# Two-block transformer on one core: the second w_out unit split during the forget-gate attention, the third unit's load issued before the recurrence

## The chip, the cores and the metric

One NeuronCore of one Trainium2 chip. The metric is the device time of one execution in microseconds (us); lower is better. The kernel before: 2402.63 us, median of three runs (2399.54, 2402.63, 2403.07).

## What is computed

Two blocks in sequence over 512 tokens of width 1024, in float32. The part that the change touches is the mixer of the first block:

```python
proj = hn @ w_in[l]
...
fox_out = fox_attention(to_heads(fq), to_heads(fk), to_heads(fv), log_f)   # 8 heads of 64, causal, forget gates
rec = hgrn2_chunkwise(gq, gf, gi, lbs[l])                                  # 4 heads of 128, gated recurrence
rec = rmsnorm(rec, hgrn_norm_g[l]) * silu(gg)
h = h + concatenate([fox_out, rec], axis=-1) @ w_out[l]                    # "out": 4 units of 256 columns
mem_n = rmsnorm(mem, norm_mem_g[l])                                        # 256 memory rows
h = h + memory_cross_attention(rmsnorm(h, norm_x_g[l]), mem_n, w_xq[l], w_xkv[l], w_xo[l])
```

After that come a squared-ReLU MLP, and the second block: pooling with grid attention, an mLSTM, and two gated MLPs.

## The kernel before, in words

Every large product runs on TensorE in three passes. A weight w is split into wH, its rounded copy, and wL = w - wH; the activation likewise (hnH and hnL, or uH and uL). `parts` (L1680) issues wH·xH, wH·xL and wL·xH. The weights are cut by `plan()` (L46) into 161 **units**, most of 1024 x 256. Units 0 to 14 are w_in (stage "in"), units 15 to 18 are w_out (stage "out"), and unit 19 is the first of w_xkv. Unit n uses buffers number n % 2 of `raw`, `wH` and `wL`, and goes through four steps on four engines:

- `load(n)`, SP (L405): a DMA of 1 MB into `raw`, once `low(n - 2)` is done, since that was the last reader of the buffer.
- `high(n)`, ACT (L610): waits for the load and for TensorE to have finished unit n - 2 (`blk_done`); copies `raw` into `wH`.
- `low(n)`, POOL (L507): waits for `high(n)`; wL = raw - wH.
- TensorE (L1691): `unit_ready` (L1687) waits for `high(n)` and `low(n)`, then come 48 matmuls of 128x512 in two blocks. DVE takes each block from PSUM.

Each engine runs its own instruction stream in order. The order in which a stream places `high`, `low` and `load` among its other work is written by hand. Around the change the order is this:

- TensorE: units 0 to 14, `attention("fox")` (L1769), the recurrence (L1886 on), unit 15, unit 16, four transposes of the normalized memory rows, unit 17, four transposes, unit 18, and then w_xkv.
- `attention("fox")` is a software pipeline of steps s = 0 to 31 (head s // 4, query block s % 4 of 128 rows), plus a drain. In step s, TensorE computes the scores of s (L1787, L1789), transposes the probabilities of s - 3 (L1836), and after each fourth step multiplies a head's probabilities with its values (L1814, eight matmuls, "values of head h"). DVE takes the row maximum of s (L1094, L1098), then scales the probabilities of s - 1 (L1103, L1104). ACT does the exponential of s (L683), and copies the transposed probabilities of s - 3 (L702) and the gates (L672). Between these, DVE prepares the recurrence through `gate_steps` (L1174): among this are four cumulative sums (L1187, TENSOR_TENSOR_SCAN), one per step from step 21 on.
- The recurrence uses PE, DVE, ACT and POOL (L527 to L536). It ends with the DVE operation that makes the last `uL` (L1029); this is counted in `op_lo`.
- SP: loads 0 to 15, then a wait for `op_lo` at the end of the attention, the table `lvl` (L441), a wait for `op_lo` at the end of the recurrence, the memory rows `mtok` (L445), and then loads 16 on (L446).
- POOL: `low(0)` to `low(15)` (L519), the recurrence, `low(16)` on (L537).
- ACT: `high(0)` to `high(15)`, the attention, the recurrence, `high(16)` (L765), the memory statistics (L766 to L769), `high(17)` (L770), `high(18)` with the memory chunks.

So unit 15 is ready long before it is used, and unit 16 is loaded and split while TensorE works on unit 15.

Of the kernel before, what the change touches and what calls it, by code (L numbers as in the profile page):

```python
# [109 lines left out]
UNITS, AT = plan()  # L110
# [58 lines left out]
def add(i, count):  # L169

    return count if i is None else i + count


def outputs(kind, t):

    h = t // TB
    if t % TB != TB - 1 or not 0 <= h < ATT[kind]["heads"]:
        return []
    return [2 * h, 2 * h + 1] if kind == "cross" else [h // 2] if h % 2 else []


def bass_block_pair(nc, a, out):
# [155 lines left out]
    with ExitStack() as ctx:  # L338
# [65 lines left out]
        def _(sp):  # L404
            def load(n, value=None, src=None):  # L405


                w, k0, kc, c0, c, _ = UNITS[n]
                if n >= 2:
                    sp.wait_ge(w_lo, (n if value is None else value) - 1)  # L410
                if src is None:
                    src = weight_view(w)[:, k0:k0 + kc, c0:c0 + c]
                sp.dma_start(raw[n % 2][:, 0:kc, 0:c], src).then_inc(raw_in[n % 2], 16)

            def loads(first, last):
                for n in range(first, last):
                    load(n)
# [19 lines left out]
            sp.dma_start(gbias[96:128, :], a["od_gate_b_2"].rearrange("a b -> b a")).then_inc(vec_in, 16)  # L437
            loads(0, AT["out"][0] + 1)

            sp.wait_ge(op_lo, Q0["mix"] + 4)  # L440
            sp.dma_start(lvl[:], a["levels"].rearrange("l s t -> s l t")).then_inc(lvl_in, 16)  # L441

            sp.wait_ge(op_lo, Q0["mix"] + 8)
            for mb in range(2):
                sp.dma_start(mtok[:, mb, :], a["mem"][0, mb * P:(mb + 1) * P, :]).then_inc(mem_in, 16)  # L445
            loads(AT["out"][0] + 1, AT["ff1"][0])  # L446

            def load_ada(layer, i, m):

# [56 lines left out]
        def _(pool):  # L506
            def low(n, value=None):  # L507

                _, _, kc, _, c, _ = UNITS[n]
                pool.wait_ge(w_hi, (n if value is None else value) + 1)  # L510
                nc.gpsimd.tensor_tensor(wL[n % 2][:, 0:kc, 0:c], raw[n % 2][:, 0:kc, 0:c],  # L511
                                        wH[n % 2][:, 0:kc, 0:c].bitcast(F32), ALU.subtract).then_inc(w_lo, 1)

            def lows(first, last):
                for n in range(first, last):
                    low(n)


            lows(0, AT["out"][0] + 1)  # L519

            v = 0
            for h in range(HG_H):
                for l in range(len(HG_LEVELS)):
# [8 lines left out]
                    if l == 3:  # L532
# [1 line left out]
                        if h:  # L534
                            pool.wait_ge(h_kt, h)
                        nc.gpsimd.tensor_tensor(kd[:], gk[:, h, :], ed[:], ALU.mult).then_inc(h_kd, 1)  # L536
            lows(AT["out"][0] + 1, AT["ff1"][0])  # L537
            n0 = AT["ff1"][0]
            with pool.Fori(0, 4) as i:
                for u in range(8):  # L540
# [60 lines left out]
        def _(act):  # L601
# [8 lines left out]
            def high(n, i=None, du=0, db=0):  # L610


                if n >= N_UNITS:
                    return
                _, _, kc, _, c, _ = UNITS[n]
                act.wait_ge(raw_in[n % 2], add(None if i is None else i * (8 * du), 16 * (n // 2 + 1)))
                if n >= 2:
                    act.wait_ge(blk_done, add(None if i is None else i * db, BLOCK0[n - 1]))
                nc.scalar.activation(wH[n % 2][:, 0:kc, 0:c], raw[n % 2][:, 0:kc, 0:c], ACT.Copy).then_inc(w_hi, 1)  # L619
# [39 lines left out]
            def attention(kind):  # L659
                c = ATT[kind]  # L660
                ns = c["heads"] * TB
                width = {"fox": None, "cross": M_MEM, "grid": S}[kind]
                for s in range(ns + 7):
                    g = c["step0"] + s
                    if kind == "fox":

                        h = 0 if s == 0 else (s + 2) // 4 if s % 4 == 2 else FOX_H
                        if h < FOX_H:
                            act.wait_ge(f_bc, h + 1)
                            if h >= 2:  # L670
                                act.wait_ge(mx_done, 4 * (h - 1))
                            nc.scalar.activation(fbc[h % 2][:], ps[2 + h % 2][:], ACT.Copy).then_inc(f_bcs, 1)  # L672
                    if s < ns:
                        i = s % TB
                        w = (i + 1) * P if kind == "fox" else width
                        act.wait_ge(mx_done, g + 1)
                        if kind == "fox":
                            src = pr[g % PR_RING][:, 0:w]
                        else:
                            src = ps[4 + g % 2][:, 0:w]  # L680
                            act.wait_ge(tp_done, g - PR_RING + 1)
                        m = g % PR_RING
                        nc.scalar.activation(pr[m][:, 0:w], src, ACT.Exp, bias=nmax[:, m:m + 1],  # L683
                                             accum_out=rsum[:, m:m + 1]).then_inc(ex_done, 1)
                    if kind == "fox" and s == 8:

                        act.wait_ge(blk_taken, TAKEN[BLOCK0[AT["out"][0]]])
                        nc.scalar.activation(gq[:], gq[:], ACT.Silu).then_inc(h_act, 1)
                        nc.scalar.activation(gg[:], gg[:], ACT.Silu).then_inc(h_act, 1)
                        nc.scalar.activation(gk[:], gk[:], ACT.Sigmoid).then_inc(h_act, 1)  # L690
                    if kind == "fox" and s == 16:
                        for hh in range(HG_H):
                            act.wait_ge(h_fk, hh + 1)
                            nc.scalar.activation(lnf[:, hh, :], lnf[:, hh, :], ACT.Ln).then_inc(h_ln, 1)
                    t = s - 3
                    if 0 <= t < ns:
                        h, i = t // TB, t % TB
                        nj = (i + 1) if kind == "fox" else width // P
                        act.wait_ge(tp_done, c["step0"] + t + 1)
                        if i == 0 and h >= 2:  # L700
                            act.wait_ge(pv_done, c["pv0"] + c["pvh"] * (h - 1))
                        nc.scalar.activation(pT[h % 2][:, 0:nj, i * P:(i + 1) * P],  # L702
                                             ps[6 + (c["step0"] + t) % 2][:, 0:nj * P].rearrange("p (j t) -> p j t", j=nj),
                                             ACT.Copy).then_inc(pt_done, 1)

                    for o in outputs(kind, s - 5):
                        act.wait_ge(pv_done, c["pv0"] + (o + 1 if kind == "cross" else 2 * o + 2))
                        nc.scalar.activation(uH[:, c["col0"] + o, :], ps[o % 2][:], ACT.Copy).then_inc(op_hi, 1)
# [14 lines left out]
            for u, n in enumerate(range(*ranges("in"))):  # L723
                high(n + 1)
                if u == 8:
# [4 lines left out]
                    nc.scalar.activation(frow[1][:], frow[1][:], ACT.Ln, bias=ones[0:FOX_H, 0:1]).then_inc(f_l, 1)  # L730

            attention("fox")

            v = 0
# [27 lines left out]
                high_op(Q0["mix"] + 4 + h, uH[:, 4 + h, :], T[h % 2][:], (op_t, tq[0]))  # L762

            n = AT["out"][0]
            high(n + 1)  # L765
            act.wait_ge(mem_in, 32)  # L766
            for mb in range(2):
                chain(nc.scalar.activation(mdump[:], mtok[:, mb, :], ACT.Square, accum_out=mstat[:, mb:mb + 1]))
            nc.scalar.activation(mstat[:, 4:6], mstat[:, 0:2], ACT.Sqrt, bias=eps, scale=1.0 / D).then_inc(m_root, 1)  # L769
            high(n + 2)  # L770
            for half in range(2):
                high(n + 3 + half)
                for j in range(4 * half, 4 * half + 4):
# [4 lines left out]
            n = AT["xkv"][0]  # L778
# [8 lines left out]
            for n in range(*ranges("xq")):  # L787
                high(n + 1)
            attention("cross")
            for n in range(*ranges("xo")):  # L790
                high(n + 1)
# [34 lines left out]
            n = AT["ev_in"][0]  # L826
# [22 lines left out]
            for j in range(2):  # L849
                act.wait_ge(g_dup, j + 1)  # L850
                nc.scalar.activation(kdup[:, j, :], ps[(7, 4)[j]][:], ACT.Copy).then_inc(g_kd, 1)
            attention("grid")
            for j in range(4):
                tq[0] += 1
# [46 lines left out]
            n = AT["od_in"][0]  # L901
# [1315 lines left out]
```

## Time and profile before

| what | us |
|---|---|
| median of three runs | 2402.63 |
| lowest and highest run | 2399.54, 2403.07 |
| profiled execution, first to last instruction (its span) | 2398.8 |
| PE busy | 2172.8 |
| DVE, POOL, ACT busy | 1170.9, 845.5, 707.7 |

Each run gives one number for the whole execution. The profiled execution has its span of 2398.8 us; no separate device time is listed for it. The median of the runs is 3.8 us above the span. Times in the rows below are from the start of the span. PE is TensorE, and its granted clock is shown as a share of 2.4 GHz: 1.00 is the upper level of 2.4 GHz, 0.50 the lower of 1.2 GHz.

### The profile page before, as it was taken

Reading aid. Unit: us, or ns where it says so; the run is one execution under the profiler, and the core shown is the slowest. Engines: PE = TensorE matmul, PEld = TensorE weight load, DVE = VectorE, ACT = ScalarE, POOL = GpSimd, SP = SyncE. Lnnn points to the kernel's source line nnn. Section 1 sums busy time; section 2 is a strip of 40 time slices with the busy share of each in tenths; the row PEclk is TensorE's granted clock in tenths of the full one; section 3 lists DMA queues with packets and bytes.
Section 4 is the critical chain, followed back from the end, with each engine's and each line's share of the span. In section 5 each row is a group of like instructions: output and inputs, shape, how many; then the busy total and the mean of one; then the engine's idle time right before and its main releaser. Section 6 shows DMA issues by size and latency. Waiting matters only on the chain.

```text
span 2398.8 us, 26469 instructions
## 1 busy us (share of the span) xinstructions
PE 2172.8 (91%) x10170; PEld 1732.0 (72%) x10170; DVE 1170.9 (49%) x1876; ACT 707.7 (30%) x938; POOL 845.5 (35%) x303
## 2 busy tenths in 40 slices
PE   6998857899889999979987999999799878999998
PEld 5884356786668788867346888888698556888887
DVE  4113695553288887463535676632456654111112
ACT  3124522333332221333433212222233332313221
POOL 2441062451324443323212443344233323344442
PEclk8997878899989999989898999999899988999999
DMA  4320001241345553312004555522232002233322
GB/s 133 97 88 0 9 1 53 89 140 53 123 136 180 175 175 125 103 53 101 0 18 140 176 176 178 189 88 88 80 96 71 1 1 88 88 97 97 98 90 75
DMA packets 220414, 226.12 MB, mean 94 GB/s; under 512 B 3787, under 2 KB 218524, under 8 KB 220188
## 3 DMA queue, kind: packets, MB, share of 16 engines
q1 hardware_dynamic: 220316, 224.78, 28.8%
q8 instruction: 65, 1.06, 0.2%
q14 instruction: 33, 0.27, 0.0%
HBM read 222.67 MB, written 2.10 MB: 94 GB/s over the span
## 4 chain that ended last, share of the span: by engine, by line
PE 76%; DVE 11%; issue 7%; ACT 4%; POOL 1%; DMA 1%; DVEq 0%; SPq 0%; ACTq 0%; POOLq 0%
PE ps L1683 22%; PE ps L1685 21%; PE ps L1684 21%; PE ps L1814 2%; PE ps L1794 1%; DVE ssum L995 1%; ACT wH L619 1%; DVE adacc L1361 1%; DVE ssum L992 1%; PE ps L1836 1%; PE ps L1898 1%; PE ps L1787 1%; PE ps L1750 1%; DVE small L1009 1%; PE ps L1805 1%
## 5 line engine op out<-in xcount | busy, mean ns | idle before, releaser
L511 POOL TENSOR_TENSOR wL<-raw,wH 128x2048 fp32r<-128x2048 f32 (+2 forms) x161 | 729.6, 4533 | 1308.1 <-ACT wH L619 1308.1
L1683 PE MATMUL ps<-hnH,wH 128*128 128x512 f32 x1336 | 530.5, 397 | 20.2 <-DVE hnL L1031 9.9
L1684 PE MATMUL ps<-hnL,wH 128*128 128x512 f32 x1336 | 525.2, 393 | 0.0
L1685 PE MATMUL ps<-hnH,wL 128*128 128x512 f32 x1336 | 525.0, 393 | 0.0
L619 ACT ACTIVATE wH<-raw 128x2048 fp32r<-128x2048 f32 (+2 forms) x161 | 302.4, 1879 | 673.7 <-PE ps L1685 653.6
L1683 PE MATMUL ps<-uH,wH 128*128 128x512 f32 x864 | 342.2, 396 | 13.7 <-DVE uL L1029 9.8
L1684 PE MATMUL ps<-uL,wH 128*128 128x512 f32 x864 | 338.9, 392 | 0.0
L1685 PE MATMUL ps<-uH,wL 128*128 128x512 f32 x864 | 338.9, 392 | 0.0
L1683 PEld LDWEIGHTS ps<-hnH,wH 128*128 128x128 f32 x1336 | 254.2, 190 | 75.1 <-issue 23.3
L1685 PEld LDWEIGHTS ps<-hnH,wL 128*128 128x128 f32 x1336 | 254.1, 190 | 54.3
L1684 PEld LDWEIGHTS ps<-hnL,wH 128*128 128x128 f32 x1336 | 254.4, 190 | 52.6 <-issue 0.5
L1361 DVE SCALAR_TENSOR_TENSOR adacc<-adaw,small,adacc 128x256 f32<-128x256 f32 x336 | 278.8, 830 | 12.0
L1683 PEld LDWEIGHTS ps<-uH,wH 128*128 128x128 f32 x864 | 163.8, 190 | 49.5 <-issue 13.6
L1487 DVE TENSOR_TENSOR T<-ps,R 128x512 f32<-128x512 f32 x44 | 30.4, 692 | 325.0 <-PE ps L1685 325.0
L1685 PEld LDWEIGHTS ps<-uH,wL 128*128 128x128 f32 x864 | 163.8, 190 | 34.8
L1684 PEld LDWEIGHTS ps<-uL,wH 128*128 128x128 f32 x864 | 163.9, 190 | 33.4
L1076 DVE SCALAR_TENSOR_TENSOR xT<-ps,mod,xT 128x512 f32<-128x512 f32 x64 | 47.4, 750 | 183.8 <-PE ps L1685 183.8
L1683 PE MATMUL ps<-wH,hnH 128*128 128x256 f32 (+1 forms) x416 | 117.7, 283 | 2.9 <-issue 2.9
L1684 PE MATMUL ps<-wL,hnH 128*128 128x256 f32 (+1 forms) x416 | 117.5, 282 | 0.0
L1685 PE MATMUL ps<-wH,hnL 128*128 128x256 f32 (+1 forms) x416 | 117.4, 282 | 0.0
L1390 DVE TENSOR_TENSOR uL<-T,uH 128x512 fp32r<-128x512 f32 x32 | 84.6, 2681 | 21.6 <-ACT uH L812 21.6
L879 ACT ACTIVATE uH<-T 128x512 fp32r<-128x512 f32 x44 | 27.8, 633 | 190.2 <-DVE T L1487 190.2
(330 smaller groups left out, 2524.5 us busy)
## 6 DMA issues: line engine op xcount, KB each, us to landing
raw<-in_ffn_w_dram SPq DMA_DIRECT2D x60, 1024.0 KB, 5.3
adaw<-in_ada_w_dram SPq DMA_DIRECT2D x48, 1024.0 KB, 7.3
raw<-in_w_dram SPq DMA_DIRECT2D x32, 1024.0 KB, 5.2
raw<-in_w_in_dram SPq DMA_DIRECT2D x14, 1024.0 KB, 5.4
raw<-in_od_w_in_dram SPq DMA_DIRECT2D x12, 1024.0 KB, 5.3
raw<-in_w_xkv_dram SPq DMA_DIRECT2D x8, 1024.0 KB, 5.2
raw<-in_ffn_w_dram SPq DMA_DIRECT2D x8, 768.0 KB, 4.2
raw<-in_ev_w_in_dram SPq DMA_DIRECT2D x5, 1024.0 KB, 5.3
```

The costliest lines, as they stand in the source:

```text
L511: nc.gpsimd.tensor_tensor(wL[n % 2][:, 0:kc, 0:c], raw[n % 2][:, 0:kc, 0:c], wH[n % 2][:, 0:kc, 0:c].bitcast(F32), ALU.subtract).then_inc( ...
L619: nc.scalar.activation(wH[n % 2][:, 0:kc, 0:c], raw[n % 2][:, 0:kc, 0:c], ACT.Copy).then_inc(w_hi, 1)
L879: nc.scalar.activation(uH[:, 2 * p + c, :], T[(q0 + c) % 2][:], ACT.Copy).then_inc(op_hi, 1)
L992: nc.vector.tensor_copy(acc[:], sq[q % 2][:]).then_inc(sq_added, 1)
L1076: nc.vector.scalar_tensor_tensor(out=xT[:, j, :], in0=ps[b % 4][:], scalar=gate(j), in1=xT[:, j, :], op0=ALU.mult, op1=ALU.add).then_inc(b ...
L1361: ins = nc.vector.scalar_tensor_tensor(out=acc, in0=adaw[m % ADA_RING][:, k, :], scalar=condc[:, k:k + 1], in1=acc, op0=ALU.mult, op1=ALU.add)
L1390: nc.vector.tensor_tensor(uL[:, 2 * u + c, :], T[q % 2][:], uH[:, 2 * u + c, :].bitcast(F32), ALU.subtract).then_inc(op_lo, 1)
L1487: nc.vector.tensor_tensor(T[(q0 + c) % 2][:], ps[b % 4][:], R[c][:], ALU.mult).then_inc(blk_taken, 1)
L1683: nc.tensor.matmul(out_ap, wh, xh, start=first, stop=False)
L1684: nc.tensor.matmul(out_ap, wh, xl, start=False, stop=False)
L1685: return nc.tensor.matmul(out_ap, wl, xh, start=False, stop=last)
L1814: ins = nc.tensor.matmul(ps[h // 2 % 2][hp:hp + 64, t0:S], v, pT[h % 2][:, j, t0:S], start=(j == 0), stop=(j == TB - 1))
```

## The change

SP issues loads 16 and 17 right behind load 15, ahead of its two waits for the attention and for the recurrence. ACT does `high(16)` in the attention, at step 20, behind the exponential of that step; behind the recurrence it does `high(17)` at once, ahead of the memory statistics instead of behind them. POOL does `low(16)` behind `low(15)`, ahead of the recurrence's operations.

```diff
@@ SP
             loads(0, AT["out"][0] + 1)
 
+            load(AT["out"][0] + 1)
+            load(AT["out"][0] + 2)
             sp.wait_ge(op_lo, Q0["mix"] + 4)
...
-            loads(AT["out"][0] + 1, AT["ff1"][0])
+            loads(AT["out"][0] + 3, AT["ff1"][0])
@@ POOL
-            lows(0, AT["out"][0] + 1)
+            lows(0, AT["out"][0] + 2)
...
-            lows(AT["out"][0] + 1, AT["ff1"][0])
+            lows(AT["out"][0] + 2, AT["ff1"][0])
@@ ACT, in attention()
+                    if kind == "fox" and s == 20:
+                        high(AT["out"][0] + 1)
                     if kind == "fox" and s == 16:
@@ ACT, behind the recurrence
             n = AT["out"][0]
-            high(n + 1)
+            high(n + 2)
             act.wait_ge(mem_in, 32)
...
-            high(n + 2)
             for half in range(2):
                 high(n + 3 + half)
```

Two lines are added above ACT's and POOL's code, so line numbers of the changed kernel are 2 to 4 higher there.

ACT in the attention, from the exponential of step 20 (`pr_86`) to that of step 21 (`pr_87`). Before:

```order
L683 ACTIVATE pr_86,small<-pr_86,small 128x128
L702 ACTIVATE pT_90<-ps 128x2x128
L708 ACTIVATE uH<-ps 128x512
L683 ACTIVATE pr_87,small<-pr_87,small 128x256
L702 ACTIVATE pT_90<-ps 128x3x128
```

With the change:

```order
L685 ACTIVATE pr_86,small<-pr_86,small 128x128
L621 ACTIVATE wH_51<-raw_49 128x2048
L706 ACTIVATE pT_90<-ps 128x2x128
L712 ACTIVATE uH<-ps 128x512
L685 ACTIVATE pr_87,small<-pr_87,small 128x256
L706 ACTIVATE pT_90<-ps 128x3x128
```

The copy of unit 16 stands between the two exponentials, ahead of a copy of transposed probabilities and of one `uH`.

ACT behind the recurrence, from its last `uH`. Before:

```order
L645 ACTIVATE uH<-T_69 128x512
L619 ACTIVATE wH_51<-raw_49 128x2048
L768 ACTIVATE mdump,small<-mtok 128x1024 x2
L769 ACTIVATE small<-small 128x2
L619 ACTIVATE wH_52<-raw_50 128x2048
L619 ACTIVATE wH_51<-raw_49 128x2048
```

With the change:

```order
L647 ACTIVATE uH<-T_69 128x512
L621 ACTIVATE wH_52<-raw_50 128x2048
L772 ACTIVATE mdump,small<-mtok 128x1024 x2
L773 ACTIVATE small<-small 128x2
L621 ACTIVATE wH_51<-raw_49 128x2048
```

`high(16)` (`wH_51`) is gone from here, and `high(17)` (`wH_52`) stands ahead of the memory statistics.

POOL, from `low(14)` to the first operations of the recurrence. Before:

```order
L511 TENSOR_TENSOR wL_53<-raw_49,wH_51 128x2048
L511 TENSOR_TENSOR wL_54<-raw_50,wH_52 128x2048
L527 TENSOR_TENSOR kt_106<-gk,R_70 128x512
L527 TENSOR_TENSOR kt_107<-gk,R_71 128x512
```

With the change:

```order
L513 TENSOR_TENSOR wL_53<-raw_49,wH_51 128x2048
L513 TENSOR_TENSOR wL_54<-raw_50,wH_52 128x2048
L513 TENSOR_TENSOR wL_53<-raw_49,wH_51 128x2048
L529 TENSOR_TENSOR kt_106<-gk,R_70 128x512
L529 TENSOR_TENSOR kt_107<-gk,R_71 128x512
```

`low(16)` is the third row: it now stands ahead of the recurrence.

## Rows read from the trace of the kernel before

**Rows 1.** The page: the span, and the chain that ended last, by engine

```profile
span 2398.8 us, 26469 instructions
...
PE 76%; DVE 11%; issue 7%; ACT 4%; POOL 1%; DMA 1%; DVEq 0%; SPq 0%; ACTq 0%; POOLq 0%
```

**Rows 2.** PE timeline, unit 15 to unit 16 (start, us, operation, [idle before <- releaser])

```profile
419.10 0.39 PE L1683 MATMUL ps<-uH,wH 128*128 128x512 f32 x1
...
421.60 0.39 PE L1685 MATMUL ps<-uH,wL 128*128 128x512 f32 x1
424.21 0.61 PE L1683 MATMUL ps<-uH,wH 128*128 128x512 f32 x1 [2.22 <-ACT wH L619]
424.62 0.63 PE L1684 MATMUL ps<-uL,wH 128*128 128x512 f32 x1
...
436.80 1.04 PE L1943 MATMUL ps<-cst,mtok 128*128 128x128 f32 x8
```

**Rows 3.** SP timeline behind the recurrence

```profile
408.70 15.80 SPq L413 DMA_DIRECT2D raw<-in_w_out_dram  x3
```

**Rows 4.** ACT timeline behind the recurrence

```profile
417.54 1.92 ACT L619 ACTIVATE wH<-raw 128x2048 fp32r<-128x2048 f32 x1 [10.45 <-DMA raw<-in_w_out_dram]
419.36 1.04 ACT L768 ACTIVATE mdump<-mtok 128x1024 f32<-128x1024 f32 x1
...
422.08 1.91 ACT L619 ACTIVATE wH<-raw 128x2048 fp32r<-128x2048 f32 x1
```

**Rows 5.** POOL timeline, from unit 15 on

```profile
188.90 4.60 POOL L511 TENSOR_TENSOR wL<-raw,wH 128x2048 fp32r<-128x2048 f32 x1 [6.31 <-ACT wH L619]
295.47 2.80 POOL L527 TENSOR_TENSOR kt<-gk,R 128x512 f32<-128x512 f32 x2 [101.98 <-ACT R L738]
...
419.54 9.54 POOL L511 TENSOR_TENSOR wL<-raw,wH 128x2048 fp32r<-128x2048 f32 x2 [36.70 <-ACT wH L619]
```

**Rows 6.** DVE timeline, the scaling of the memory rows

```profile
422.82 6.81 DVE L1316 TENSOR_SCALAR mtok<-mtok,small 128x1024 f32<-128x1024 f32 x2
```

**Rows 7.** ACT timeline in the attention: exponentials of steps 20 and 21, copy of 19

```profile
262.04 0.40 ACT L683 ACTIVATE pr<-pr,small 128x128 f32<-128x128 f32 x1 [4.62 <-DVE small L1098]
...
264.24 0.51 ACT L683 ACTIVATE pr<-pr,small 128x256 f32<-128x256 f32 x1 [0.95 <-DVE small L1098]
...
267.62 0.58 ACT L702 ACTIVATE pT<-ps 128x512 f32<-128x512 f32 x1
```

**Rows 8.** DVE timeline in the attention, steps 21 to 24

```profile
264.52 1.22 DVE L1187 TENSOR_TENSOR_SCAN gb<-rmask,lnf 128x512 f32<-128x512 f32 x1
...
266.24 0.55 DVE L1094 CUSTOM_DVE_ANT_0 pr<-ps,fbc 128x384 f32<-128x384 f32 x1
...
267.08 0.35 DVE L1104 TENSOR_SCALAR pr<-pr,small 128x256 f32<-128x256 f32 x1
...
272.75 0.29 DVE L1094 CUSTOM_DVE_ANT_0 pr<-ps,fbc 128x128 f32<-128x128 f32 x1 [1.51 <-PE ps L1789]
```

**Rows 9.** PE timeline in the attention: values of head 3 and of head 4

```profile
256.61 4.30 PE L1814 MATMUL ps<-pT,fv 128*64 128x512 f32 x8 [0.98 <-ACT pT L702]
...
268.80 3.33 PE L1814 MATMUL ps<-pT,fv 128*64 128x512 f32 x8
```

**Rows 10.** Two DVE lines over the whole run (min/median/max ns, first and last start)

```profile
L1361 DVE SCALAR_TENSOR_TENSOR adacc<-adaw,small,adacc x336: 483/485/4865, 677.9 to 1577.3; 128x256 f32<-128x256 f32 x168
...
L1098 DVE TENSOR_SCALAR small<-small x80: 153/154/155, 200.7 to 1222.3; 128x1 f32<-128x1 f32 x80
```

**Rows 11.** DVE and POOL timelines where a scan and a subtraction met

```profile
154.67 1.21 DVE L1166 TENSOR_TENSOR_SCAN frow<-cst,frow 8x512 f32<-8x512 f32 x1
...
154.96 5.34 POOL L511 TENSOR_TENSOR wL<-raw,wH 128x2048 fp32r<-128x2048 f32 x1 [6.28 <-ACT wH L619]
```

**Rows 12.** Windows of two heads: length, PE, PEld, DVE, ACT, POOL busy, clock, DMA

```profile
257.00:269.00 12.00, 12.00 (x33) 4.80 (x32) 6.16 (x19) 4.33 (x14) 0.00 (x0) 0.64 0.00 1
...
278.20:286.00 7.80, 7.32 (x31) 3.50 (x32) 5.28 (x25) 4.29 (x13) 0.00 (x0) 1.00 0.00 0
```

## Prediction, made before the changed kernel ran

> **What bounds the kernel now.** I first read the page's chain of waits: three quarters of what ended last is PE [rows 1]. So time is won where PE stands still, and lost where it is made to. The first place the change speaks of is the seam between units 15 and 16, in PE's timeline [rows 2]. The last matmul of unit 15 starts at 421.60, the first of unit 16 at 424.21, with 2.22 us idle. Behind that two matmuls start 0.41 us apart (424.21, 424.62), where those of unit 15 came every 0.227 us (eleven from 419.10 to 421.60): PE is at its lower clock level, 1.2 GHz, for some matmuls.
>
> Why PE waited is in SP's, ACT's and POOL's timelines. Load 16 goes out at 408.70, with the end of the recurrence [rows 3]. ACT waits 10.45 us for it and copies at 417.54 [rows 4]. POOL takes 419.54 to about 424.1 for the subtraction: two of them make the 9.54 us of the row [rows 5]. PE starts 0.1 us later, so POOL's subtraction, not the copy named in the row, released it.
>
> The second place is where the work goes to: the attention, steps 20 to 24. POOL is idle for 101.98 us there [rows 5], and ACT has gaps. But DVE has not many, and I read its timeline [rows 8] for what a POOL instruction would do to it.
>
> **The change, part by part.**
>
> *The seam (gain).* With wH and wL of unit 16 ready, its first matmul follows at the pace of unit 15, at 421.60 + 0.23 = 421.83 instead of 424.21: 2.38 us. Unit 16 lasted from 424.21 to 436.80 (the transposes), 12.59 us; 48 matmuls at 0.227 us are 10.88. That gives another 1.71 us, if PE keeps the upper level. Sum: **-4.1 us**. Bounds: -2.4, if the clock falls anyway, and -4.1.
>
> *Is something late next?* ACT's `high(17)` now stands ahead of the memory statistics, and it waits for PE to finish unit 15, at 422.0. Before, it started at 422.08 for the same reason, so `low(17)` isn't later: 424.0 to 428.7, while unit 17 is needed at 421.83 + 10.88 + 0.8 (transposes) = 433.5. The statistics, 419.36 to 422.0 in rows 4, move to 423.9 to 426.6. DVE waits for them and then scales the memory rows. Before, this pair took 6.81 us, from 422.82 to 429.6, beside two POOL subtractions [rows 5, 6]. Now it starts at 426.7, and if it is held until POOL ends at 428.7 it is done by 430.2 at the latest. PE asks for it at 432.7. So there are 2.5 us to spare: cost 0. DVE is 1 to 3 us late for the first block of unit 16, which nobody needs before unit 18.
>
> *SP.* Loads 16 and 17 pass the two waits and the loads of `lvl` and `mtok`. They run at 185 to 200, where DMA is idle after that until the recurrence (a share of 0.00) [rows 12]. `mtok` and load 18 follow at 408 with less beside them. Cost 0.
>
> *ACT in the attention.* The copy takes 1.91 us [rows 4], from 262.44 (262.04 + 0.40) to 264.35, between the exponentials of steps 20 and 21. ACT had 0.95 us idle ahead of the latter [rows 7], so that one comes 1.0 us late, at 265.25. DVE uses its sum only after 266.2. Cost of this alone: 0; if DVE had no slack, 1.0.
>
> *POOL in the attention (loss).* `low(16)` starts 0.08 us behind the copy (417.54 + 1.92 against 419.54), at 264.43, and takes 4.60 us [rows 4, 5], to 269.03. The trace shows what DVE does under such an instruction. The line L1361 (two SBUF tensors) takes 0.485 us in the median and 4.865 at most [rows 10]: the longest ones stood beside a subtraction of 4.6 us, and waited for all of it. L1098, on one column, never takes over 0.155. The scaling of rows 6 was held too. Operations that read PSUM, as L1094 does, were not lengthened beside a subtraction anywhere.
>
> So which of DVE's operations fall into 264.43 to 269.03? The first cumulative sum, due at 264.52, and the scaling of step 21, due at 267.08 [rows 8]. For the scan the trace has one meeting: a scan started at 154.67, a subtraction at 154.96, and the subtraction took 5.34 us instead of 4.60, which is the rest of the scan [rows 11]. So they exclude each other, and who comes first goes first. Here POOL comes 0.09 us ahead. The bounds for the hold of DVE: 0, and 4.6 us.
>
> The Trainium skill's "GPSIMD Engine Reference", section "Specifications", says that GpSimd shares its SBUF interfaces with VectorE, with contention for VectorE instructions that have two SBUF inputs or run in a 2-port performance mode. The scan (`rmask`, `lnf`) has two SBUF inputs and the scaling would be of the other kind, so by this rule both are held, and the change gives the +0.8 us of the sum below; were nothing held, it would give the -4.1 us of the seam. Rows 10 agree with it (4.865 against 0.485 us).
>
> I take the hold in full, as rows 11 are the nearest: the scan waits from 264.52 to 269.03, 4.5 us. Everything behind it on DVE moves by that: the maximum of step 22 from 266.24 to 270.75, and on ACT its exponential and the copy of step 19, from 267.62 to 272.1, done at 272.7 [rows 7, 8]. PE needs that copy for the values of head 4, which began at 268.80 [rows 9]. PE stands still until 272.7: **+3.9 us**. The eight matmuls took 3.3 us in part at the upper level; those of head 3, at the lower one throughout, took 4.30 [rows 9]. After 4 us idle I count the lower: **+1.0**. Behind them DVE had waited 1.51 us for PE (272.75), and has its backlog done by then, so nothing is added and little comes back. Sum of the loss: **+4.9 us**, with bounds of 0.1 and, if the lower level lasts, 10.9 (below).
>
> *Sum.* -4.1 + 4.9 = **+0.8 us** on the profiled span of 2398.8, so 2399.6. The median of the runs stands 3.8 us above that span: 2402.6 + 0.8 = **2403.4 us**. Two effects of some 4 to 5 us cancel.
>
> **The rivals.**
>
> *B. The scan comes first.* The order rests on 0.09 us. If the scan wins, POOL waits to 265.73 and runs to 270.33. The scan and the maximum of step 22 are on time, and so is PE's head 4. The scaling of step 21, due at 267.08, waits 3.25 us. The gap of 1.51 us at 272.75 and smaller ones take up half; head 5's values come 1.5 us late. -4.1 + 1.5 = -2.6: 2400.0 us. For it: a tenth of a microsecond is little. Against: ACT and DVE are both timed by the same scores.
>
> *C. The scan isn't held.* Then only the scaling waits, from 267.08 to 269.03, 1.95 us, and the gap at 272.75 takes up most: +0.3. -4.1 + 0.3 = -3.8: 2398.8 us. For it: no row shows a 128-partition scan under a running subtraction. Against: rows 11.
>
> *D. Slower, by the clock.* PE's pause in head 4 brings the clock down, and the pipeline's gaps keep it there. Head 3's stretch at a granted clock of 0.64 takes 12.0 us; the next ones take 9.2 (269.0 to 278.2) and 7.8 at 1.00 [rows 12]. If both run as the first, they cost 2.8 + 4.2 = 7.0, of which 1.0 is counted: the loss is 10.9, the sum +6.8, 2409.4 us. It decides where the granted clock between 277 and 287 stays near 0.64. Against: head 3's own pauses did not stop the clock from rising to 1.00 two heads on.
>
> That the change doesn't do what it says is hardly possible: `high(16)` waits only for a load landed by 200 and for unit 14.
>
> **How the numbers follow.** A (the sum) 0.60, B 0.15, C 0.15, D 0.10. The runs before span 3.5 us, so each case gets about 2 us either way; A's own range is 2401 to 2406. A measurement of this kernel can tell about 0.2%, 4.8 us, from no change: below 2397.8 is faster, above 2407.4 slower. No case but C is near the first (a third of it, and a little of B): 0.07. The second takes most of D and a tail of A: 0.09. The rest, 0.84, is the same. The range, 2397.8 to 2407.6, takes in C and B and leaves out most of D and the tails.
>
> **What would show it.** (1) Unit 16 follows unit 15 within 0.3 us, and lasts 10.9 us at clock 1.00. (2) The first scan (now L1189) shows some 5.7 us instead of 1.22, or, by B, the second scaling behind it shows 3.6; by C the scan stays at 1.22 and the scaling shows 2.3. (3) PE waits about 4 us for `pT` ahead of the values of head 4. (4) The recurrence starts 4 to 5 us later than before, and unit 17 0.5 to 1 us later. (5) No wait of PE ahead of the memory transposes. I am wrong if the seam keeps an idle of over 1 us, if the clock drops there all the same, or if the attention is as long as before.

## The result and the profile after

The changed kernel takes **2405.57 us** (median of 20 runs, 2403.65 to 2407.21), the kernel before took 2399.88 us in the same comparison (20 runs, 2397.56 to 2403.71). The ratio is 1.0023 with a 95% interval of 1.0016 to 1.003, so the change is **5.7 us slower**, clear of no change. The forecast was 2403.4 us, which is +0.8 us on a kernel before of 2402.6, and "the same" within about 0.2%, 4.8 us.

The time lies inside the range, 2397.8 to 2407.6. That is in part luck: the kernel before took 2.75 us less here than the 2402.63 us that the forecast was built on, and the same +5.7 us on top of 2402.63 would have been 2408.3, outside the range. The difference itself was forecast too small, +0.8 instead of +5.7 us, and it exceeds the 4.8 us that the prediction took as the limit of "the same".

One of the 29 runs of the kernel before that stand beside e9 to e11 took 3252.75 us, at a mean clock of 0.622, and is left out of the ratios.

The profiled execution after has a span of 2401.9 us. Its device time is 2403.65 us, the fastest of the 20, 1.75 us above the span. Its span is 3.1 us above that of [rows 1]. By stage, from starts that both traces show:

| stretch | before, us | after, us | difference |
|---|---|---|---|
| attention, to the first `kt` of the recurrence | ends 295.47 | ends 303.27 | +7.8 |
| recurrence, to the first matmul of unit 15 | 112.48 | 111.93 | -0.55 |
| first matmul of unit 15 to that of unit 17 | 29.65 | 25.21 | -4.4 |
| the rest | | | +0.3 |

Unit 17 starts at 440.41 instead of 437.60. Of the -4.4 us, 4.1 lie between the last matmul of unit 15 and the transposes, as shown next.

**The seam**, in the PE timeline of after, columns as in [rows 2]:

```profile
428.51 0.39 PE L1688 MATMUL ps<-uH,wL 128*128 128x512 f32 x1
428.74 0.39 PE L1686 MATMUL ps<-uH,wH 128*128 128x512 f32 x1
...
439.62 1.04 PE L1946 MATMUL ps<-cst,mtok 128*128 128x128 f32 x8
```

The first matmul of unit 16 (L1686) starts 0.23 us after the last of unit 15 (L1688), with no idle between. Unit 16 lasts 10.88 us (428.74 to 439.62) where it lasted 12.59 [rows 2]. From the last matmul of unit 15 to the transposes it was 421.60 to 436.80, 15.20 us. Now it is 428.51 to 439.62, 11.11 us: -4.1 us. The memory rows are scaled by 436.8, in time for the transposes at 439.62. DVE's timeline of after (before: [rows 6]):

```profile
433.69 3.13 DVE L1319 TENSOR_SCALAR mtok<-mtok,small 128x1024 f32<-128x1024 f32 x2
```

**POOL**, timeline of after (before: [rows 5]). The subtraction of unit 16 stands in the attention now:

```profile
264.20 4.55 POOL L513 TENSOR_TENSOR wL<-raw,wH 128x2048 fp32r<-128x2048 f32 x1 [70.78 <-ACT wH L621]
303.27 2.79 POOL L529 TENSOR_TENSOR kt<-gk,R 128x512 f32<-128x512 f32 x2 [34.52 <-ACT R L742]
```

**DVE** beside it, timeline of after (before: [rows 8]):

```profile
264.30 5.53 DVE L1190 TENSOR_TENSOR_SCAN gb<-rmask,lnf 128x512 f32<-128x512 f32 x1
269.75 0.66 DVE L1032 TENSOR_TENSOR uL<-ps,uH 128x512 fp32r<-128x512 f32 x1
270.33 0.54 DVE L1097 CUSTOM_DVE_ANT_0 pr<-ps,fbc 128x384 f32<-128x384 f32 x1
```

The scan shows 5.53 us instead of 1.22. Its record starts 0.10 us behind that of POOL's subtraction. POOL ends at 268.75, and the scan ends at 269.83, 1.08 us later, near the 1.22 that it takes alone. So the scan waited for the subtraction to end. The maximum of step 22 starts at 270.33 instead of 266.24, 4.1 us later.

**PE** there, timeline of after (before: [rows 9] for heads 3 and 4; heads 5 and 6 began at 278.2 and 285.7 with 2.37 us each):

```profile
266.21 0.28 PE L1839 MATMUL ps<-cst,pr 128*128 128x128 f32 x1
272.35 4.53 PE L1817 MATMUL ps<-pT,fv 128*64 128x512 f32 x8 [5.86 <-ACT pT L706]
284.43 3.92 PE L1817 MATMUL ps<-pT,fv 128*64 128x512 f32 x8
293.52 2.37 PE L1817 MATMUL ps<-pT,fv 128*64 128x512 f32 x8 [0.48 <-ACT pT L706]
```

And the windows of after, columns as in [rows 12], the last but one the granted clock:

```profile
257.00:266.40 9.40, 9.40 (x32) 3.95 (x30) 3.97 (x11) 4.67 (x12) 2.20 (x1) 0.83 0.00 0
266.40:272.30 5.90, 0.09 (x1) 0.00 (x0) 5.83 (x8) 1.19 (x3) 2.35 (x1) 0.85 0.01 3
272.30:280.00 7.70, 7.65 (x21) 3.30 (x21) 4.92 (x14) 1.74 (x6) 0.00 (x0) 0.67 0.00 0
280.00:288.30 8.30, 8.30 (x21) 3.23 (x20) 3.27 (x15) 3.63 (x10) 0.00 (x0) 0.59 0.00 1
288.30:300.00 11.70, 10.30 (x46) 5.08 (x46) 5.53 (x23) 5.70 (x16) 0.00 (x0) 1.00 0.00 0
```

PE stands for 5.86 us. Then it is busy nearly all the time, but the granted clock averages 0.67 and 0.59 until 288.3. It falls twice in that stretch: cut finer, it is 0.50 from 272.35 to 276.9, 0.98 from 277.5 to 280.9, and 0.50 again from 280.9 to 284.4.

The delay grows from one head's values to the next: head 4's come 3.55 us later (268.80 to 272.35), head 5's 6.2 us (278.2 to 284.43), head 6's 7.8 us (285.7 to 293.52). The recurrence begins 7.8 us late.

### The profile page after: what moved, and what is told of

The parts are those of the page before. It is cut to its first block, busy times and chain, and to the rows that moved or that the text cites. A ratio compares the mean times of both kernels' runs of the same rounds, so it can differ in the third digit from the quotient of the medians.

```text
span 2401.9 us, 26469 instructions
## 1 busy us (share of the span) xinstructions
PE 2176.1 (91%) x10170; PEld 1735.7 (72%) x10170; DVE 1172.0 (49%) x1876; ACT 707.3 (29%) x938; POOL 844.7 (35%) x303
## 4 chain that ended last, share of the span: by engine, by line
PE 76%; DVE 11%; issue 7%; ACT 4%; POOL 1%; DMA 0%; DVEq 0%; SPq 0%; ACTq 0%; POOLq 0%
PE ps L1686 22%; PE ps L1688 22%; PE ps L1687 22%; PE ps L1817 2%; PE ps L1797 1%; DVE ssum L998 1%; DVE adacc L1364 1%; DVE ssum L995 1%; PE ps L1839 1%; PE ps L1901 1%; ACT wH L621 1%; PE ps L1790 1%; DVE small L1012 1%; PE ps L1753 1%; PE ps L1808 1%
## 5 line engine op out<-in xcount | busy, mean ns | idle before, releaser
L1686 PE MATMUL ps<-hnH,wH 128*128 128x512 f32 x1336 | 530.2, 397 | 20.3 <-DVE hnL L1034 9.9
L1688 PE MATMUL ps<-hnH,wL 128*128 128x512 f32 x1336 | 525.5, 393 | 0.0
L1686 PE MATMUL ps<-uH,wH 128*128 128x512 f32 x864 | 341.4, 395 | 10.2 <-DVE uL L1032 8.4
L1688 PE MATMUL ps<-uH,wL 128*128 128x512 f32 x864 | 338.5, 392 | 0.0
L1686 PEld LDWEIGHTS ps<-hnH,wH 128*128 128x128 f32 x1336 | 254.5, 191 | 75.0 <-issue 23.2
L1688 PEld LDWEIGHTS ps<-hnH,wL 128*128 128x128 f32 x1336 | 254.0, 190 | 54.2
L1364 DVE SCALAR_TENSOR_TENSOR adacc<-adaw,small,adacc 128x256 f32<-128x256 f32 x336 | 278.9, 830 | 12.0
L1686 PEld LDWEIGHTS ps<-uH,wH 128*128 128x128 f32 x864 | 163.6, 189 | 45.3 <-issue 12.3
L1688 PEld LDWEIGHTS ps<-uH,wL 128*128 128x128 f32 x864 | 163.3, 189 | 34.7
L1686 PE MATMUL ps<-wH,hnH 128*128 128x256 f32 (+1 forms) x416 | 117.8, 283 | 2.9 <-issue 2.9
L1688 PE MATMUL ps<-wH,hnL 128*128 128x256 f32 (+1 forms) x416 | 117.5, 282 | 0.0
```

What stands on the lines that cost most here:

```text
L1364: ins = nc.vector.scalar_tensor_tensor(out=acc, in0=adaw[m % ADA_RING][:, k, :], scalar=condc[:, k:k + 1], in1=acc, op0=ALU.mult, op1=ALU.add)
L1686: nc.tensor.matmul(out_ap, wh, xh, start=first, stop=False)
L1688: return nc.tensor.matmul(out_ap, wl, xh, start=False, stop=last)
```

## The experiments

Every comparison has its own runs of the kernel before. Medians are in us, with the number of runs in brackets. The recorded ratio is not exactly the quotient of the two medians, so the text says which of the two a difference comes from.

| run | median | before | ratio, 95% interval |
|---|---|---|---|
| e1_loads_only | 2395.6 (12) | 2399.87 (35) | 0.9983, 0.9973 to 0.9993 |
| e2_copy_only | 2406.39 (12) | 2399.87 | 1.002, 1.0011 to 1.003 |
| e3_split_low | 2401.56 (12) | 2399.87 | 1.0007, 0.9998 to 1.0017 |
| e4_scans_later | 2401.35 (12) | 2399.87 | 1.0002, 0.9993 to 1.0011 |
| e5_before_scans_later | 2401.44 (11) | 2398.66 (27) | 1.0017, 1.0007 to 1.0026 |
| e6_copy_only_clean | 2397.04 (11) | 2398.66 | 0.9988, 0.9979 to 0.9997 |
| e7_pool_only | 2402.58 (11) | 2398.66 | 1.0019, 1.0007 to 1.003 |
| e8_pe_kept_busy | 2407.83 (5) | 2398.66 | 1.0039, 1.0025 to 1.0053 |
| e9_pe_filled_3 | 2401.47 (11) | 2399.86 (29) | 1.0002, 0.9993 to 1.0012 |
| e10_step_30 | 2401.72 (12) | 2399.86 | 1.0006, 0.9992 to 1.0021 |
| e11_loads_high17_first | 2396.91 (11) | 2399.86 | 0.9988, 0.9976 to 1.0 |
| e12_change_again | 2406.52 (7) | 2398.84 (11) | 1.0029, 1.0018 to 1.004 |

**The loads alone**, on the kernel before: SP issues loads 16 and 17 early; ACT and POOL stay.

```diff
-            loads(0, AT["out"][0] + 1)
+            loads(0, AT["out"][0] + 3)
...
-            loads(AT["out"][0] + 1, AT["ff1"][0])
+            loads(AT["out"][0] + 3, AT["ff1"][0])
```

> Edit: only SP's part of the change: loads 16 and 17 go out behind load 15; high(16), low(16) and high(17) stay behind the recurrence as before. Theory 1 (the loss is DVE's hold under low(16) in the attention and what PE's clock does behind it): high(16) starts near 407 instead of 417.5, low(16) is done near 414, while DVE is idle; unit 16 follows unit 15 without a pause, unit 16 lasts 10.9 us, the attention is as before: 4.1 us less than before (some 8 to 10 us less than the change). Rival theory 2 (the seam's gain needs the split in the attention): as before within 1 us. If PE's clock falls at the seam all the same: 2.4 us less than before.

It gains 4.3 us by the medians, 4.1 by the ratio. Its timelines of ACT, POOL and PE at the seam:

```profile
407.57 1.89 ACT L619 ACTIVATE wH<-raw 128x2048 fp32r<-128x2048 f32 x1
...
409.54 4.56 POOL L511 TENSOR_TENSOR wL<-raw,wH 128x2048 fp32r<-128x2048 f32 x1 [26.12 <-ACT wH L619]
...
422.17 0.39 PE L1685 MATMUL ps<-uH,wL 128*128 128x512 f32 x1
422.40 0.39 PE L1683 MATMUL ps<-uH,wH 128*128 128x512 f32 x1
```

With the data there, copy and subtraction are done at 414.1, 8.3 us before PE asks. So the whole gain at the seam comes from issuing the loads ahead of the recurrence. Preparing unit 16 in the attention adds nothing to it. **This version beats both kernels.**

**The copy alone**, on the changed kernel: POOL's `low(16)` goes back behind the recurrence, ACT's `high(16)` stays at step 20.

```diff
-            lows(0, AT["out"][0] + 2)
+            lows(0, AT["out"][0] + 1)
...
-            lows(AT["out"][0] + 2, AT["ff1"][0])
+            lows(AT["out"][0] + 1, AT["ff1"][0])
```

> Edit: the change, but low(16) behind the recurrence's POOL work instead of ahead of it; high(16) stays at step 20 of the attention. Theory 1: the copy alone costs the attention 0 to 1 us, the first scan stays at 1.2 us, PE doesn't wait for pT for more than 2 us ahead of head 4's values; low(16) runs near 383 to 388, where DVE reads PSUM; total 3 to 4 us less than before. Rival theory 3 (it is the copy on ACT, not POOL, that delays the attention): the attention stays 4 us or more longer, total as before or slower.

A miss, and a useful one. The copy being ready, POOL went on right behind its last product of the recurrence, not behind the recurrence. Its POOL and DVE timelines:

```profile
387.28 4.52 POOL L513 TENSOR_TENSOR wL<-raw,wH 128x2048 fp32r<-128x2048 f32 x1
```

```profile
388.71 3.64 DVE L1222 TENSOR_TENSOR sq<-gq,dd 128x512 f32<-128x512 f32 x1
```

The same product of two SBUF tensors takes 0.68 us in the kernel before (L1219). From the first `kt` (299.75) to unit 15 it took 119.65 us, 7.2 more than before (112.48). Up to POOL's last product, `gsum`, the two are alike (299.75 to 386.06, 86.3 us, and 295.47 to 381.57, 86.1), so the loss lies behind it. The hold of the product is 3.0 us of it. Another 3.2 us lie in PE's 32 one-column matmuls that follow: 6.9 us at a granted clock of 0.50, where the kernel before took 3.7 us at 1.00. The edit put the subtraction in a second bad place, and its total says nothing of the copy.

**The copy alone, with POOL kept away**, the edit of e2 and a wait for the end of the recurrence:

```diff
+            pool.wait_ge(op_lo, Q0["mix"] + 8)
+            lows(AT["out"][0] + 1, AT["ff1"][0])
```

> Edit: the change, with low(16) behind a wait for the end of the recurrence (op_lo), when DVE has nothing to do; high(16) stays at step 20. e2 had put low(16) into the last products of the recurrence, where it held DVE. Theory 1: total 3 to 4.5 us less than before, as e1, because the copy on ACT costs 0 to 1 us. Theory 3 (the copy on ACT upsets the pipeline and PE's clock): 1 us less than before up to 5 us more.

Timelines of ACT, DVE and PE of this run:

```profile
262.55 1.90 ACT L622 ACTIVATE wH<-raw 128x2048 fp32r<-128x2048 f32 x1
```

```profile
264.62 1.22 DVE L1191 TENSOR_TENSOR_SCAN gb<-rmask,lnf 128x512 f32<-128x512 f32 x1
```

```profile
268.92 3.31 PE L1818 MATMUL ps<-pT,fv 128*64 128x512 f32 x8
```

The copy is there, the scan and the values of head 4 are as before, and the recurrence starts at 295.58 (before 295.47). In these two traces the copy costs 0.1 us. By the ratio the kernel gains 2.9 us, 1.2 less than e1 and a little less than was expected, but the intervals overlap.

**POOL's work alone**, on e1: a subtraction of the same size at the same place, whose result is overwritten by the real one, and no copy on ACT.

```diff
             lows(0, AT["out"][0] + 1)
+            pool.wait_ge(raw_in[0], 16 * ((AT["out"][0] + 1) // 2 + 1))
+            pool.wait_ge(blk_done, BLOCK0[AT["out"][0]])
+            pool.wait_ge(mx_done, 22)
+            nc.gpsimd.tensor_tensor(wL[0][:], raw[0][:], raw[0][:], ALU.subtract)
```

> Edit: e1 (loads early, all else as before), plus one POOL subtraction of 128x2048 into the free buffer wL[0], whose result nobody uses, started by the maximum of step 21: POOL's hold alone, without the copy on ACT. Theory 1: it starts near 264.3, the first scan shows over 5 us, PE waits 4 to 6 us ahead of head 4's values, and the total is that of the change, 8 to 10 us above e1 (4 to 6 above before). Theory 3 (the copy on ACT is what costs): within 2 us of e1.

Timelines of POOL, DVE and PE:

```profile
267.38 3.67 POOL L523 TENSOR_TENSOR wL<-raw 128x2048 fp32r<-128x2048 f32 x1 [73.87 <-DVE small L1102]
```

```profile
267.52 4.62 DVE L1191 TENSOR_TENSOR_SCAN gb<-rmask,lnf 128x512 f32<-128x512 f32 x1
```

```profile
274.66 4.53 PE L1818 MATMUL ps<-pT,fv 128*64 128x512 f32 x8 [5.00 <-ACT pT L706]
```

Against e1 one POOL instruction turns 0.9983 into 1.0019, some 8.6 us. By the totals, then, the copy alone costs nothing that was measured, and POOL's instruction alone costs the whole loss. This subtraction reads `raw` twice and is shorter, and the scan's record is shorter with it: 4.62 us instead of 5.53. Its trace shows less of the loss than the total does: it was 3 us late already ahead of POOL's instruction, as is taken up below under "The sum".

**What is held: the scan, by its place.** In e4 (on the change) and e5 (on the kernel before) the scans come four steps of the generator later.

```diff
-                for _ in range(6):
+                for _ in range(10):
```

> Edit: the change, with the four cumulative sums on DVE four steps later (steps 25 to 28), out of low(16)'s way. Theory 1: nothing but the scaling of step 21 is held, for some 2 us; PE's pause ahead of head 4's values is under 1.5 us, the attention loses 0 to 2 us against the same kernel without the change's moves; total 2 to 4 us less than that kernel. Rival theory 3 (the copy on ACT): the loss stays at 5 us or more.

> Edit: the kernel before, with the four cumulative sums four steps later (steps 25 to 28) and nothing else: the base of e4. Theory 1: this alone costs 1 to 4 us in heads 6 and 7, so that e4 (1.5 us above before) stands 1 us or more below this base, of which the seam gives 4.1 and the held scaling and the clock take back the rest. If this kernel is as fast as before (within 1 us), e4's attention still loses about 5 us with no scan held, and theory 1 doesn't explain the loss alone.

DVE and POOL timelines of e4:

```profile
268.03 2.54 DVE L1107 TENSOR_SCALAR pr<-pr,small 128x256 f32<-128x256 f32 x1
```

```profile
265.86 4.56 POOL L513 TENSOR_TENSOR wL<-raw,wH 128x2048 fp32r<-128x2048 f32 x1 [71.27 <-ACT wH L621]
```

Now the scaling of step 21 is held, 2.54 us instead of 0.35. The recurrence starts at 300.39, 0.9 us later than in its base e5 (299.50), where the change lost 7.8. Even these 0.9 us were there before, at the values of head 3 (258.0 and 257.1). So a scaling held for 2.2 us cost nothing in this trace. Against e5 the change is then a gain of some 3.6 us by the ratios, whose intervals just touch, and 2.4 us by the spans (2397.0, 2399.4). But moving the scans costs the kernel before 4.1 us by the ratio (2.8 by the medians), so this isn't the way.

**The subtraction in four pieces**, on the change:

```diff
+                if n == AT["out"][0] + 1 and value is None:
+                    for k in range(0, KC, 2):
+                        ins = nc.gpsimd.tensor_tensor(wL[n % 2][:, k:k + 2, 0:c], raw[n % 2][:, k:k + 2, 0:c],
+                                                      wH[n % 2][:, k:k + 2, 0:c].bitcast(F32), ALU.subtract)
+                    ins.then_inc(w_lo, 1)
+                    return
```

> Edit: the change, with low(16) cut into four subtractions of 128x512, 1.2 us each. Theory 1: DVE's scan and scaling get in between the pieces; no DVE operation is held for over about 1.3 us, the first scan shows under 2.6 us, PE's pause ahead of head 4's values falls from 5.9 us to under 3, and the attention loses 1 to 3 us instead of 7.8; total between 3 us less than before and the same. If DVE is held across all four pieces, the loss is that of the change, 5 to 6 us slower than before.

Timelines of DVE, POOL and PE, then two windows of this run:

```profile
264.60 2.29 DVE L1196 TENSOR_TENSOR_SCAN gb<-rmask,lnf 128x512 f32<-128x512 f32 x1
```

```profile
264.50 5.95 POOL L515 TENSOR_TENSOR wL<-raw,wH 128x512 fp32r<-128x512 f32 x4 [71.08 <-ACT wH L627]
```

```profile
269.41 4.53 PE L1823 MATMUL ps<-pT,fv 128*64 128x512 f32 x8 [0.52 <-ACT pT L712]
```

```profile
264.00:269.00 5.00, 4.88 (x11) 1.69 (x11) 4.86 (x12) 3.36 (x10) 4.50 (x3) 0.51 0.01 3
269.00:278.20 9.20, 8.79 (x25) 3.81 (x26) 7.87 (x19) 2.77 (x10) 1.45 (x2) 0.69 0.00 0
```

The same two windows of the kernel before:

```profile
264.00:269.00 5.00, 5.00 (x12) 1.87 (x12) 4.74 (x14) 2.65 (x7) 0.00 (x0) 0.50 0.01 3
269.00:278.20 9.20, 8.90 (x33) 3.73 (x32) 6.68 (x23) 4.36 (x13) 0.00 (x0) 0.90 0.00 0
```

The scan waits for one piece (2.29 us, not 5.53), PE stands 0.52 us instead of 5.86, and the values of head 4 come at 269.41, 0.6 us later than before. So DVE waits to the end of the *instruction* that POOL is in. Yet the values take 4.53 us, those of head 5 3.88, and the recurrence starts at 300.29: +4.8 us, where 1 to 3 were expected. Before, the clock was just as low at 264 to 269 (0.50) and then rose (0.90); here it averages 0.69 over the same stretch, and only behind the values of head 5 does it stay at 1.00. So most of that loss isn't a pause, it is the lower clock through two heads.

**The pause filled.** On the change, PE multiplies operands that it has, with results that nobody reads, ahead of the values of head 4: ten such products in e8 and three in e9.

```diff
+                    if kind == "fox" and h == 4:
+                        pe.wait_ge(op_lo, c["q0"] + h // 2 - 1)
+                        for _ in range(3):
+                            nc.tensor.matmul(ps[0][0:64, :], fv[:, 0, 0:64], fv[:, 1, :], start=True, stop=True)
```

> Edit: the change, with ten more matmuls of 128x512 on PE (result overwritten) in the pause ahead of head 4's values: the hold stays, PE's pause is filled. Theory 1 with the clock as its second part: the scan is held as in the change, the values of head 4 take 2.4 us instead of 4.5 and those of head 5 2.4 instead of 3.9, at granted clock near 1.00; total 3 to 4 us less than the change, 1 to 3 above before. If the part behind the hold isn't the clock's: as the change, or 1 to 2 us slower.

> Edit: as e8, but three more matmuls instead of ten, 3 to 6 us of PE work, so that the pause of 5.9 us is filled and not overrun. Theory 1 with the clock as its second part: the scan is held as in the change; the values of head 4 start within 1 us of the change's 272.4 and take 2.4 to 3.5 us instead of 4.5; the attention loses 6 to 7 us instead of 7.8; total 0.5 to 2 us less than the change. Head 5's stretch at the lower level need not go away, since e8 still had it. If the clock behind the pause doesn't depend on the pause, the values of head 4 take 4.5 us as in the change.

PE timeline of e8: ten products (20 records) overran the pause, to 278.9, so its total (9 us above before, where 1 to 3 were expected) says little. The values of head 4 were fast, and those of head 5 were not, though PE had not paused.

```profile
269.30 9.75 PE L1805 MATMUL ps<-fv 128*64 128x512 f32 x20
278.89 2.32 PE L1821 MATMUL ps<-pT,fv 128*64 128x512 f32 x8
...
288.46 3.98 PE L1821 MATMUL ps<-pT,fv 128*64 128x512 f32 x8
```

e9, the PE timeline and windows:

```profile
269.67 2.79 PE L1805 MATMUL ps<-fv 128*64 128x512 f32 x6
275.60 2.37 PE L1821 MATMUL ps<-pT,fv 128*64 128x512 f32 x8 [3.14 <-ACT pT L706]
284.01 2.37 PE L1821 MATMUL ps<-pT,fv 128*64 128x512 f32 x8 [0.29 <-ACT pT L706]
...
275.60:284.00 8.40, 8.11 (x32) 3.62 (x32) 7.17 (x24) 4.35 (x13) 0.00 (x0) 1.00 0.00 0
284.00:291.50 7.50, 7.07 (x30) 3.33 (x30) 5.02 (x22) 4.29 (x13) 0.00 (x0) 1.00 0.00 1
```

The hold is untouched (the scan shows 5.54 us) and PE still waits, but the clock stays at 1.00, and a head takes 8.4 and 7.5 us where the change takes 12.1 and 9.1. The ratio falls from 1.0023 to 1.0002, some 5 us (each against its own runs of before, and the intervals are apart). A gain of 0.5 to 2 us was expected.

The trace to compare with is that of e7, which was as late ahead of the hold (values of head 3 at 259.7 in both) and has no filling. From the values of head 4 to the recurrence e7 takes 28.4 us (274.66 to 303.09) and e9 25.7 (275.60 to 301.30). So filling the pause is worth 2.7 us by this pair of traces and some 5 us by the totals. So a good part of the loss is the clock's, though the two figures don't agree on how large a part.

**Another place**, on the change: `high(16)` at step 30 instead of 20.

```diff
-                    if kind == "fox" and s == 20:
+                    if kind == "fox" and s == 30:
```

> Edit: the change, with high(16) at step 30 instead of 20, behind the four scans, at the last steps of the attention. Theory 1: low(16) still holds DVE's scalings of steps 30 or 31, whose result PE's transposes wait for: one DVE record of 3 to 5 us, a pause of PE of 2 to 5 us, the attention 2 to 6 us longer than before and the total between 2 us less and 3 us more than before, in any case above e1. If only the scans were the trouble: as e1, 4 us less than before.

Its timelines of DVE, POOL and PE:

```profile
292.52 3.45 DVE L1107 TENSOR_SCALAR pr<-pr,small 128x512 f32<-128x512 f32 x1
```

```profile
291.19 4.51 POOL L513 TENSOR_TENSOR wL<-raw,wH 128x2048 fp32r<-128x2048 f32 x1 [97.69 <-ACT wH L621]
```

```profile
291.64 4.53 PE L1817 MATMUL ps<-pT,fv 128*64 128x512 f32 x8 [2.28 <-ACT pT L706]
```

No scan is near, but a scaling is held instead, and the values of head 6 fall to the lower level. By the ratios this is better than step 20 by some 4 us, though the intervals overlap, and still no gain over before. At both places that were tried DVE had something that POOL holds.

**The order of the statistics**, on e1: `high(17)` moved ahead of the wait for the memory rows, as the change has it.

```diff
             high(n + 1)
+            high(n + 2)
             act.wait_ge(mem_in, 32)
...
-            high(n + 2)
```

> Edit: e1, with high(17) ahead of the memory statistics on ACT, as the change has it. Theory 1: it costs nothing, since the memory rows are scaled 2.5 to 3 us before PE asks for them: as e1 within 1 us, 3 to 4.5 us less than before; PE goes from unit 16 to the transposes without a wait. Rival theory 4 (part of the loss is there): 2 us or more above e1.

PE goes from unit 16 at 432.06 to the transposes at 432.30, without a wait; 0.9988 against 0.9983 is no difference that was measured, so this order costs nothing that shows.

**The change once more**, with no edit, in the company of other runs:

> Edit: none, the changed kernel once more, for a second profiled execution; the first was the fastest of its 20 runs. In the traces so far the attention ran in two ways up to step 20 (values of head 3 at 256.4 to 257.7, or at 259.6 to 259.7), whatever the kernel. Theory 1 with the clock: with the scan held, the recurrence starts at 303 to 304 in either way, 7.5 us behind the first way of an unheld kernel and 3.5 behind its second; total 4 to 6 us above before. If this execution is slower than 2404.5 us, its trace shows where the first one was fast.

The ratio is 1.0029 beside the 1.0023 of the first time, 7.0 us, a little more than the 4 to 6 expected. The scan is again 5.53 us, 0.10 us behind POOL. The values of head 4 come at 273.2 with 4.53 us, those of head 5 at 285.3 with 3.93, the recurrence at 304.14. So the hold isn't a chance of one profile. The span is 1.0 us above that of the first profile, and 0.8 of it were there at the values of head 3 (257.2 and 256.4).

## Where the prediction was right and where it was wrong

- **The seam, -4.1 us: right**, by its steps. 2.38 of pause, and unit 16 in 10.88 us. What it didn't ask is whether the load alone would give it. It did (e1: -4.3 us).
- **Copy on ACT, order of the statistics, SP: 0, right.** e6, e11 and e1, each on its own. PE asks for the memory rows at 439.6; they were scaled at 436.8: 2.8 us to spare, 2.5 predicted.
- **Who comes first, and what is held: right.** POOL ahead by 0.10 us (0.09 predicted), in both profiles of the change; the scan is held in full. Rivals B and C fell with that. C would have had a scaling of 2.3 us held, which is what e4 shows (2.54) once the scan is out of the way.
- **The wait of PE, +3.9: nearly right.** The values of head 4 came 3.55 us later. The pause shows 5.86 us, since PE did the work ahead of it faster (from 257 to 266.4 at clock 0.83, before at 0.68), which bought nothing.
- **The lower clock, +1.0: the term that failed.** The prediction charged the eight matmuls of head 4 and said that behind them "nothing is added and little comes back". They took 4.53 us instead of 3.33 (+1.2, near the 1.0). But then part of head 5's scores ran at the lower level too (+1.5 us up to its values: 6.2 less 3.55 and 1.2), and head 5's values and what follows added another 1.6 (7.8 less 6.2). So 3.55 + 1.2 + 1.5 + 1.6 = 7.8 us instead of 4.9. Rival D priced the lower clock through two heads at 10.9 us. The loss in the trace lies half-way between the sum and D, and the measured +5.7 us is nearer to D's +6.8 than to +0.8. The step that failed was to take head 3's stretch [rows 12] only as the bound and not as the nearest row. Its clock had gone the same way, low, high and low again (0.54 from 256.6 to 260.9, 1.00 to 263.8, 0.52 to 268.8), and it had lasted a head and more.
- **The sum.** The traces say +3.1 us, the medians +5.7. The profiled execution of before, at 2398.8 + 1.75 us, is 0.7 above its median, and that of the change is 1.9 below its own. Part of this may come from how the attention runs up to step 20. It goes in one of two ways, and the code up to there does not decide it: the change and e10 are the same up to step 20 and went different ways. These are the windows of e7 and of the kernel before:

```profile
240.00:250.00 10.00, 10.00 (x25) 3.82 (x26) 7.25 (x27) 4.88 (x14) 0.00 (x0) 0.66 0.00 1
```

```profile
240.00:250.00 10.00, 8.60 (x37) 3.91 (x36) 7.04 (x27) 5.35 (x14) 0.00 (x0) 1.00 0.00 1
```

Call the way of the kernel before, at 1.00, the first, and that of e7, at 0.66, the second. In the second way (e2, e7, e9, e10) head 3's values start at 259.6 to 259.7, in the first, which all other traces took, at 256.4 to 258.0. Kernels with the scans in place and no subtraction in the attention began the recurrence at 295.5 to 296.6 in the first way (before, e1, e6, e11), and at 299.75 in the second (e2). With the hold it is 303.3 and 304.1 in the first (the change, twice) and 303.1 in the second (e7). So the hold cost 7.8 us in the first way and 3.3 us in the second (e7 against e2, with a hold 0.9 us shorter), and with it the two ways end alike. In the second way the kernel without a hold had its slow values at head 5 (3.75 us, head 4 at 2.37), the one with a hold at head 4 (4.53, head 5 at 2.37). If the runs of before are a mix of the two ways, this would make the runs of the change lie closer together and higher, as they do (2403.65 to 2407.21, against 2397.56 to 2403.71). It is argued from single profiles, not shown. It doesn't explain the 2 us by which the usual run of the change exceeds its profiled one either. The mean clock goes with it: the three runs of the change at 2403.65 to 2403.77 us have a mean granted clock of 0.939 to 0.940, the other 17 one of 0.936 to 0.938. No trace held one of those, so where they lose it **stays open**, as does what starts the second way.

## What to carry to other kernels

Ask of a preparation that is moved which of its three steps was late. Here only the DMA was: moving it alone gave 0.9983, and with the other two steps moved along it was 1.0023. An idle POOL is no free place for a big subtraction. Look at what DVE reads from SBUF beside it, and count the hold as up to the length of POOL's instruction. When an edit makes TensorE pause in a stretch where its granted clock is already seen to waver, count with the lower clock for up to two heads (4.2 us in the change), and not only for the next eight matmuls.

## What the runs showed of the hardware

- DVE's scans, scalings and products of SBUF tensors took turns with POOL's subtractions, by whole instructions: a scan took 5.53 us (1.22 alone) beside a subtraction of 4.55, 4.62 beside one of 3.67, and 2.29 beside a piece of 1.3. POOL's lead was 0.10 us in the change. POOL is held as well: among the four pieces of e3 the second, with the scan beside it, took 2.18 us and the others 1.26 to 1.31. The Trainium skill's "GPSIMD Engine Reference", section "Specifications", names the shared SBUF interface and the kinds of DVE instructions that contend for it; scan and scaling (2.54 against 0.35 us in e4) agree with that. How long each waited is read from the rows.
- Not held: the maxima that read PSUM, as the one of step 22 in e4 (267.18, 0.55 us, while POOL's subtraction ran from 265.86 to 270.42), and beside it operations on one column, at 0.15 us.
- The length of a pause alone does not tell what the granted clock does behind it. In e9 PE did 2.79 us of extra matmuls and then paused 3.14 us, and the clock was 1.00 behind it. In the change PE came into its pause of 5.86 us at the upper level (1.00 from 264 to 266.4) and left it at the lower (0.50 from 272.35 to 276.9). It was back at 0.98 from 277.5 to 280.9 and fell again to 0.50 from 280.9, with no pause ahead of that second fall. In e8, too, the clock fell from 1.00 (278.9 to 284.9) to 0.54 (284.9 to 292.4) with PE busy throughout. In e3 there was a pause of 0.52 us, the clock was low ahead of it, as before, and stayed low for longer. These runs say no more of it.
